# Opening of a two-layer diffusion backbone: paired squares, root, first rows and filter pieces put in another order

## The reference, cut to what matters

```python
s_lat = silu(c); s_ctx = silu(c_ctx)
sh1, sc1, ... = split(s_lat @ w_mod[l] + b_mod[l])            # and mod_c from s_ctx
xn  = rmsnorm(h,  norm1_g[l]) * (1 + sc1)  + sh1
xnc = rmsnorm(hc, norm1_g[l]) * (1 + sc1c) + sh1c             # rmsnorm: x * rsqrt(mean(x*x) + EPS) * g
proj = xn @ w_in[l]                                           # 1024 -> 512 + 1536 + 384 + 288 + 3072
# filter of the long convolution, both layers', from the parameters alone
hid = sin(freq1 * (z @ w1 + b1))
hid = sin(freq2 * (hid @ w2 + b2))
h   = (hid @ w3).reshape(L, 2, 512) * exp(-t * abs(decay))
```

## Time and profile before

| | |
|---|---|
| median of three runs | 1478.03 us (1476.47 to 1479.28) |
| profiled execution, its own time | 1475.15 us |
| its span (first to last instruction) | 1473.3 us |
| TensorE busy | 1396.2 us, 95% |
| VectorE, ScalarE, GpSimd busy | 759.2, 555.1, 204.0 us |
| mean granted TensorE clock | 0.98 of 2.4 GHz |

### The profile page before, as it was taken

One profiled execution on the slowest core, in us unless ns is written; L12 is line 12 of the kernel. 1 busy time (PEld: TensorE's weight loads), 2 busy tenths in 40 slices (PEclk: granted clock), 3 DMA queues, 4 the chain that ended last, 5 costly groups with the idle time before them and its releaser, 6 DMA issues.

```text
span 1473.3 us, 19582 instructions
## 1 busy us (share of the span) xinstructions
PE 1396.2 (95%) x8082; PEld 1125.4 (76%) x8082; DVE 759.2 (52%) x1055; ACT 555.1 (38%) x859; POOL 204.0 (14%) x189
## 2 busy tenths in 40 slices
PE   6889999999999999799999999988999999899996
PEld 3546766777777787577777777766868989899996
DVE  5253756324453464644333443346775767675664
ACT  5434355233232231533212332115464544564551
POOL 1142100241101134000000000210003302400012
PEclk9899999999999999899999999999999999999998
DMA  9222220444641134244444445422314654456562
GB/s 379 98 76 99 86 86 33 175 171 145 228 143 57 46 105 177 102 150 150 171 143 164 150 151 171 150 90 76 129 58 151 215 200 148 139 191 196 192 197 70
DMA packets 56377, 208.43 MB, mean 141 GB/s; under 512 B 6261, under 2 KB 7669, under 8 KB 54752
## 3 DMA queue, kind: packets, MB, share of 16 engines
q1 hardware_dynamic: 53600, 194.22, 38.4%
q0 software_dynamic: 2688, 12.95, 2.3%
HBM read 203.48 MB, written 3.67 MB: 141 GB/s over the span
## 4 chain that ended last, share of the span: by engine, by line
PE 91%; DVE 4%; ACT 3%; issue 1%; DMA 1%; POOL 0%; DVEq 0%; ACTq 0%; POOLq 0%
PE ps L1376 26%; PE ps L1377 25%; PE ps L1378 25%; PE ps L1405 3%; PE ps L1658 2%; PE ps L1756 1%; PE ps L1766 1%; PE ps L1516 1%; PE ps L1669 1%; PE ps L1682 1%; ACT normed L684 1%; PE ps L1534 1%; DVE rstd L974 1%; DVE wl L937 1%; PE ps L1504 1%
## 5 line engine op out<-in xcount | busy, mean ns | idle before, releaser
L1376 PE MATMUL ps<-xh,wh 128*128 128x512 f32 (+2 forms) x1376 | 475.9, 346 | 36.2 <-DVE xl L984 34.1
L937 DVE TENSOR_TENSOR wl<-raw,wh 128x1024 fp32r<-128x1024 f32 (+2 forms) x272 | 355.6, 1310 | 236.4 <-ACT wh L652 233.2
L1377 PE MATMUL ps<-xl,wh 128*128 128x512 f32 (+2 forms) x1376 | 468.0, 340 | 0.0
L1378 PE MATMUL ps<-xh,wl 128*128 128x512 f32 (+2 forms) x1376 | 467.5, 340 | 0.0
L652 ACT ACTIVATE wh<-raw 128x1024 fp32r<-128x1024 f32 (+2 forms) x272 | 283.5, 1043 | 317.4 <-PE ps L1378 315.9
L1376 PEld LDWEIGHTS ps<-xh,wh 128*128 128x128 f32 (+1 forms) x1376 | 261.5, 190 | 81.2 <-issue 36.6
L1378 PEld LDWEIGHTS ps<-xh,wl 128*128 128x128 f32 (+1 forms) x1376 | 261.7, 190 | 31.0
L1377 PEld LDWEIGHTS ps<-xl,wh 128*128 128x128 f32 (+1 forms) x1376 | 261.8, 190 | 30.0 <-issue 1.3
L1376 PE MATMUL ps<-hid_h,wh 128*128 128x512 f32 (+1 forms) x512 | 172.0, 336 | 0.0
L1377 PE MATMUL ps<-hid_l,wh 128*128 128x512 f32 (+1 forms) x512 | 170.6, 333 | 0.0
L1378 PE MATMUL ps<-hid_h,wl 128*128 128x512 f32 (+1 forms) x512 | 170.3, 333 | 0.0
(11 more groups left out here) (224 smaller groups left out, 1446.3 us busy)
## 6 DMA issues: line engine op xcount, KB each, us to landing
raw<-in_units SPq DMA_DIRECT2D x262, 512.0 KB, 3.4
mod_ring<-in_mod_units SPq DMA_DIRECT2D x80, 512.0 KB, 4.0
pairs<-in_pairs SPq DMA_DIRECT2D x6, 1024.0 KB, 13.1
filters<-filt POOLq DMA_DIRECT2D x10, 256.0 KB, 2.6
filt<-filters POOLq DMA_DIRECT2D x2, 1280.0 KB, 10.0
ftab<-in_fwd POOLq DMA_DIRECT2D x3, 768.0 KB, 5.1
raw<-in_units SPq DMA_DIRECT2D x6, 384.0 KB, 2.9
h<-in_x SPq DMA_DIRECT2D x4, 512.0 KB, 8.0
```

Of the source, the lines that this page charges most:

```text
L937: dve.tensor_tensor(wl[:, g % SLOTS, 0:n], raw[:, g % SLOTS, 0:n], wh[:, g % SLOTS, 0:n].bitcast(F), ALU.subtract)\
L1376: pe.matmul(dst, w_h, m_h, start=first, stop=False)
L1377: pe.matmul(dst, w_h, m_l, start=False, stop=False)
L1378: return pe.matmul(dst, w_l, m_h, start=False, stop=last)
```

## The change

It does six things, all in the opening:

- The four additions of squares all run on VectorE, the first ahead of the first sine argument, the others behind it. GpSimd has none.
- ScalarE takes the root ahead of the first sine, copies pair 0 ahead of the first two splits, takes the first sine behind them, and splits units 2 and 3 behind the first block's norm_hi. The second sine comes behind block 2, the envelopes behind blocks 3 and 6.
- VectorE forms the first block's low part ahead of the rests of units 1 to 3, the product with the root two blocks ahead, and the second sine argument behind block 1.
- TensorE issues filter piece m - 3 in step m (from m = 3), and three pieces behind the loop instead of two. VectorE weights piece m - 4 from m = 4, and four behind the loop.
- TensorE multiplies a tile of zeros ten times (`warm(5)`, two passes each) as soon as VectorE has cleared it; `warm(4)` and the later `warm(5)` become `warm(2)` and `warm(3)`.
- The second filter multiply moves behind pair(1) and warm(3), directly ahead of the wave.

```diff
@@ -346,7 +346,7 @@
         pair_done, pair_copied, pair_turned = sem("pair_multiplied"), sem("pair_rows_copied"), sem("pair_rows_turned")
         pair_added, pair_ready = sem("pair_added"), sem("pair_ready")
         x_squared, x_full = sem("x_squared"), sem("x_full_ready")
-        x_paired_pool, x_paired_dve = sem("x_paired_by_gpsimd"), sem("x_paired_by_vector")
+        x_paired, idle_clear = sem("x_paired"), sem("idle_tile_clear")
         mod_loaded = sems("mod_unit_loaded", MOD_SLOTS)
         mod_done = sem("mod_unit_multiplied")
         mod_copied = sem("mod_rows_copied")
@@ -509,9 +509,6 @@
             pool.wait_ge(h_in_s[3], 16)
             pool.dma_start(f_w3[:, :], f_w3_in).then_inc(f_w3_in_s, 16)
             pool.dma_start(decay[:, :], decay_in[0:1, :].broadcast_to([128, 2 * HY])).then_inc(decay_in_s[0], 16)
-            for c in range(2):
-                pool.wait_ge(x_squared, 2 * c + 2)
-                pool.tensor_tensor(normed[:, 2 * c, :], normed[:, 2 * c, :], normed[:, 2 * c + 1, :], ALU.add).then_inc(x_paired_pool, 1)
             pool.wait_ge(pair_loaded[1], 16)
             pool.dma_start(ftab0[:, :, :], fwd_in).then_inc(ftab_in_s, 16)
 
@@ -754,23 +751,24 @@
 
             for m in range(KB):
                 first_square(m)
-            filter_sines(0)
             std(0)
+            copy_pair(0)
             for g in range(2):
                 split(g)
-            copy_pair(0)
-            for g in range(2, WAVE):
-                split(g)
+            filter_sines(0)
             for m in range(KB):
                 norm_full(0, m)
                 norm_hi(0, m)
+                if m == 0:
+                    for g in range(2, WAVE):
+                        split(g)
                 if m + 1 < KB:
                     copy_pair(m + 1)
-                if m == 0:
+                if m == 2:
                     filter_sines(1)
-                elif m == 1:
+                elif m == 3:
                     filter_envelope(0)
-                elif m == 4:
+                elif m == 6:
                     filter_envelope(1)
 
             def first_square_of(j):
@@ -1054,31 +1052,38 @@
 
             dve.memset(small[:, 1:2], 0.0).then_inc(dve_bank_free, 2)
             dve.memset(silu_wide[:, :, :], 0.0).then_inc(silu_clear, 1)
+            dve.memset(sq_sum[:, :], 0.0).then_inc(idle_clear, 1)
             dve.wait_ge(silu_sig, 1)
             dve.wait_ge(silu_clear, 1)
             dve.tensor_tensor(silu_wide[:, :, 0:2], silu[:, :, :], param("c", KB, 2), ALU.mult).then_inc(silu_ready, 1)
+            def pair_squares(c):
+                dve.wait_ge(x_squared, 2 * c + 2)
+                dve.tensor_tensor(normed[:, 2 * c, :], normed[:, 2 * c, :], normed[:, 2 * c + 1, :], ALU.add).then_inc(x_paired, 1)
+
+            pair_squares(0)
             filter_sine_argument(0)
-            for c in range(2, 4):
-                dve.wait_ge(x_squared, 2 * c + 2)
-                dve.tensor_tensor(normed[:, 2 * c, :], normed[:, 2 * c, :], normed[:, 2 * c + 1, :], ALU.add).then_inc(x_paired_dve, 1)
+            for c in range(1, 4):
+                pair_squares(c)
             norm_rstd(0)
             norm_by_rstd(0, 0)
-            for g in range(2):
-                split(g)
             add_pair(0)
-            for g in range(2, WAVE):
+            split(0)
+            norm_by_rstd(0, 1)
+            norm_lo(0, 0)
+            for g in range(1, WAVE):
                 split(g)
             for m in range(KB):
-                if m + 1 < KB:
-                    norm_by_rstd(0, m + 1)
-                norm_lo(0, m)
+                if m:
+                    norm_lo(0, m)
                 if m + 1 < KB:
                     add_pair(m + 1)
-                if m == 0:
+                if m + 2 < KB:
+                    norm_by_rstd(0, m + 2)
+                if m == 1:
                     filter_sine_argument(1)
-                elif m >= 2:
-                    filter_weighted(m - 2)
-            for i in (6, 7):
+                elif m >= 4:
+                    filter_weighted(m - 4)
+            for i in range(4, 8):
                 filter_weighted(i)
             for layer in range(DEPTH):
                 n = width(layer)
@@ -1492,6 +1497,13 @@
                 loop(layer, "gate_" + b, main)
 
 
+            def warm(count):
+
+                for _ in range(count):
+                    pe.matmul(ps[:, 0, :], sq_sum[:, 0:128], sq_sum[:, :], start=True, stop=True)
+
+            pe.wait_ge(idle_clear, 1)
+            warm(5)
             pe.wait_ge(sine_in_s, 32)
             pe.matmul(ps[:, 7, 0:SEQ], f_w12[0:HY_EMB, 0, :], emb[0:HY_EMB, :], start=True, stop=True).then_inc(f_pre, 1)
 
@@ -1528,26 +1540,18 @@
             pe.wait_ge(act_bank_free, 2)
             pe.wait_ge(dve_bank_free, 2)
             pe.wait_ge(consts_in_s, 16)
-            def warm(count):
-
-                for _ in range(count):
-                    pe.matmul(ps[:, 0, :], ones, consts[:, 384:384 + 2 * SEQ], start=True, stop=True)
-
-            warm(4)
+            warm(2)
             for c in range(4):
-                if c < 2:
-                    pe.wait_ge(x_paired_pool, c + 1)
-                else:
-                    pe.wait_ge(x_paired_dve, c - 1)
+                pe.wait_ge(x_paired, c + 1)
                 mm = pe.matmul(ps[:, SUMSQ_BANK[0], :], ones, normed[:, 2 * c, :], start=c == 0, stop=c == 3)
             mm.then_inc(sumsq_ready, 1)
-            pe.wait_ge(f_sin, 1)
-            pe.matmul(ps[:, 7, 0:SEQ], f_w12[:, 1, :], f_hid[:, :], start=True, stop=True).then_inc(f_pre, 1)
             pe.wait_ge(silu_ready, 1)
             pair(0)
             turn_pair(0)
             pair(1)
-            warm(5)
+            warm(3)
+            pe.wait_ge(f_sin, 1)
+            pe.matmul(ps[:, 7, 0:SEQ], f_w12[:, 1, :], f_hid[:, :], start=True, stop=True).then_inc(f_pre, 1)
             first = [(g, WAVE_BANKS[g]) for g in range(WAVE)]
             for m in range(KB):
                 if m + 1 < KB:
@@ -1555,12 +1559,12 @@
                 wave_step(0, m, first, T, (x_split, 0))
                 if m + 2 < KB:
                     pair(m + 2)
-                if m == 2:
+                if m == 3:
                     pe.wait_ge(f_w3_in_s, 16)
                     pe.wait_ge(f_sin, 2)
-                if m >= 2:
-                    filter_taps(m - 2)
-            for i in (6, 7):
+                if m >= 3:
+                    filter_taps(m - 3)
+            for i in range(5, 8):
                 filter_taps(i)
 
             def first_kv():
```

## The result

The four runs of the changed kernel took 1457.70 to 1460.87 us, median **1458.33 us**. The kernel before, in the same comparison, took 1475.74 to 1479.28, median 1477.25. The ratio is 0.9874, 95% interval 0.9857 to 0.9892: faster by 1.3%, some 19 us. The forecast was 1460.0, range 1454 to 1467.

What follows compares the result with a forecast made beforehand. TensorE was taken as the bound, holding the chain of waits for 91% of the span. Opening 1.5 plus wave 18.2 less 1.7 gave 18.0 us off the 1478.0 median: 1460.0 us, range 1454 to 1467.

Steps and rivals of the forecast that it cites:

- The stuck head: In the wave, VectorE's weighting waits for a filter piece ahead of the needed low part: five TensorE waits, 9.6 us.
- The wave's length: First wave multiply to last filter piece: 43.8 us if the clock never falls, 18.2 less than 61.97.
- One slow stretch: One stretch at lower clock remains in the wave, placed at block 4's gap: 1.7 us lost, bounds 0 to 5.1.
- The opening: Ahead of the wave: first wave multiply at 28.5 us, 1.5 us earlier; bounds 26.6 and 29.6.
- Zeros: Ten early TensorE passes between some 1.7 and 8 us: free, or 0.3 us late, covered by the constants' arrival.
- Table loads: ScalarE's loads cost 1.28 us without the Trainium skill's 1.38 us drain; with it, block 4's gap would be 2.5, not 1.1.
- The sum: Whole kernel: opening and wave together gain 18.0 us, taking the profiled execution from 1475.15 to 1457.2 us.
- Rival 1: Wave: remaining gaps lower the clock repeatedly, five or six slow stretches; gain about 10 us, 1468; chance 0.12.
- Rival 2: Wave: ScalarE's chain or VectorE's second sine argument sets the pace of two more blocks; gain 13 to 15, 1464; chance 0.15.
- Rivals 3 and 4: Wave: TensorE stays at 1.2 GHz, 1484, chance 0.02; or pieces are bound otherwise, only the opening gains, 1477, chance 0.03.

Runs made afterwards that it cites:

- e5: The kernel before with only filter pieces m - 3 on TensorE and their weighting m - 4 on VectorE: 1463.28 us, ratio 0.9904.
- e6: The changed kernel with TensorE's filter piece m - 2 and VectorE's weighting m - 3, both one block earlier: 1456.12 us, repeated 1456.57 us.
- after_again: The changed kernel run once more, unchanged, as yardstick for further versions: 1459.38 us, ratio 0.9870.
- e4: The changed kernel with the first two additions of squares back on GpSimd: 1458.29 us, ratio 0.9869.
- e2: The changed kernel with the wave's old order, keeping the new opening: 1473.85 us, ratio 0.9967.
- e7: The changed kernel with each envelope shared out over ScalarE's free time in several blocks: 1457.11 us, ratio 0.9869.
- e3: The changed kernel without the five early multiplies of the zero tile, warm(2) and warm(3) kept: 1459.02 us, ratio 0.9861.
- e8: The changed kernel with the second pair loaded before the first two weight units and copied before units 2 and 3 are split: 1460.63 us, ratio 0.9877.
- e9: The changed kernel with the edits of e7 and e8 together: 1459.11 us, ratio 0.9862.

## Why the prediction was right, point by point

- **The stuck head.** The mechanism was as told. e5 shows that the distance of one block between the two queues, without anything else, gives 15.9 of the wave's 18.3 us, and e6 that it is the distance and not the later block.
- **The wave's length.** Predicted 43.8 us at full clock, with 40.6 busy; measured 43.67 and 40.77. The gaps: 0.45 each in blocks 1 to 3 (measured 0.50 each); 1.1 in block 4 (0.83); 0.7 in block 7 (0.56). The last piece ended at 71.06 and not near 74, since the wave began 1.1 us earlier than put down and the slow stretch fell behind it.
- **One slow stretch.** I had put 1.7 us of it at block 4. In the profiled execution it fell just behind the wave, in the spectra, and cost the 1.7 there (7.08 against 5.39). In after_again it fell at block 4 (granted 0.53 from 48.90 to 52.50), and in e4 nowhere up to the latents' sums. The size was right, the place varies from run to run; that it comes at all was no certainty.
- **The opening.** In the profiled execution this term was too small: 1.5 us predicted, 2.7 measured. The step that was off is "I take 1.2 GHz for most of" the six passes of warm(3): 5.0 us were assumed, 3.32 measured on the chain. The clock rose about 1 us after they began (granted 0.50 from 23.40 to 24.00, 1.00 from 24.60 on). The other way went pair(1): put down as ending at 22.7, it was itself at half clock and ended at 23.43. But this size varies: in e2, e6 and e7, with the same opening, the six passes take 4.4 to 4.7 us and the wave begins at 28.5 to 28.8, where the prediction had it. The sum of squares ended at 16.26, inside 15.5 to 17.3. ScalarE was ready for turn_pair(1) at 26.3, as summed (near 26.0), but the cover was 0.7 us and not 2, since TensorE came earlier. So VectorE doing all four additions is not quite free of consequence: in e4 the turn waits 2.1 us for ScalarE, and the wave begins 1.1 us later.
- **Zeros.** Worth nothing, as predicted; they ran from 1.75 to 9.12, longer than the 8 assumed, and put off the first filter multiply from 8.27 (e3) to 9.04, which the constants' arrival covers (TensorE still waits 1.1 us for them).
- **Table loads.** In the profile after, the exponential's load at 42.73 takes 1.28 us and the exponential begins at 44.03. The sine's load at 19.62 is followed by the sine at 20.91. The root's, at 13.51, can't tell, since ScalarE waits for TensorE behind it. The rows again show no drain of 1.38 us, and the gap of block 4 was 0.8, not the 2.5 that the prediction worked out with the drain of the Trainium skill, ScalarE: Activation LUTs, section What ACT_TABLE_LOAD costs.
- **The sum.** 18.0 us predicted for the profiled execution, 17.1 measured; 18.9 between the medians. The opening's extra 1.2 was given back late in the kernel, where the profile of after lost 2.2 us on that of before, 1.3 of it by slower 256-column multiplies (last section). Neither was in the sum. So the close total owes something to luck: two errors that cancel.
- **The rivals.** Rival 1 needed five slow stretches in the wave; of twelve profiles with late pieces only that of e8, which entered it at half clock, shows more than one, and seven show none. Rival 2 half came: ScalarE does hold the wave after the change, by 2.9 us in all (its copies 2.3, and 0.6 for a low part that waited for its high part), but no more than the 3.15 of the sum. Rivals 3 and 4 are out by the rows of the stretches.

## What to carry to other kernels

When an engine idles in front of a cheap instruction, ask what stands behind it in its queue. An instruction that consumes another engine's late result should be placed one whole step after the one that produces it; here two edits of an index gave some 13 of 19 us. An edit that only brings a step forward pays up to the next late arrival (here a transfer landing at 21.5 us), and moving that transfer ahead of others makes those late for a queue that cannot pass them. A gap costs twice where the clock falls behind it: here the wave lost 9.0 us of idle time and a further 9.3 us through the higher clock.

## What the runs showed of the hardware

**Two rates of the same multiply at full clock.** In layer 1 the products have 256 columns. TensorE waits for nothing there, and the granted clock is 1.00 in both of the following profiles. Yet the distance from one multiply to the next is 113 ns in some stretches and 118 in others, for a hundred microseconds and more. These are the multiplies of one line from 1300 to 1440 us, in the profile of after (count, busy us, mean ns of one, idle):

```profile
L1381 PE MATMUL ps<-hid_h,wh 128*128 128x256 f32 x248 | 68.4, 276 | 0.0
```

And in that of e7:

```profile
L1386 PE MATMUL ps<-hid_h,wh 128*128 128x256 f32 x233 | 65.5, 281 | 0.0
```

The busy time of one is 276 and 281 ns; from 1300 to 1440 us TensorE runs 1238 multiplies in after and 1191 in e7. From 1285 us to the end e7 loses 6.2 us on after at a constant rate, 3.9%, and the profile of e9 loses the same. A shorter stretch of it lies at 1100 to 1150 us in the profile of after, where before has 113 ns in most of the same work, and accounts for 1.3 of the 2.2 us by which the gain shrinks. What sets the rate is open: the code of these stretches is the same in all these kernels, and no row names a wait. For reading results it means that an edit of the first 70 us can seem to cost 6 us by what happens at the end.

**VectorE's additions are slow beside those of GpSimd.** A VectorE addition of 128 x 512 takes 0.68 us alone and up to 3.30 beside GpSimd's additions, and a rest of a weight unit 4.09 instead of 1.22 (after, at 73.22 us, beside GpSimd's sums). GpSimd's own took 1.28 and 1.29 beside the first of these and up to 1.71 in the wave of after. The first was on the way to the wave, as e4 shows; no wait of TensorE stands behind the second in the profile of after.
